# Moving the three steps of the merge statistics to earlier places on VectorE and ScalarE

## The reference, cut to what matters

```python
for g, (window, dil) in enumerate(DILATION_PAIRS):          # (128,1), (512,4), (2048,16)
    o, l = _dilated_group(qkv[:, :, g, 0], qkv[:, :, g, 1], qkv[:, :, g, 2], window, dil, slopes)
    outs.append(o)                                          # l = max + log(sum of exponentials)
    lses.append(l)
wts = jax.nn.softmax(jnp.stack(lses, axis=-1), axis=-1).astype(h.dtype)
o = jnp.einsum('bshg,bshgd->bshd', wts, jnp.stack(outs, axis=3))
y = o.reshape(bsz, s, A_WIDTH) * jax.nn.silu(gate)
return y @ w_out
```

## Time and profile before

| | |
|---|---|
| median of 3 runs | 2000.37 us (1996.89 to 2004.60) |
| the profiled execution, its own time | 2000.56 us |
| its span, first to last instruction | 1998.8 us |
| TensorE busy in the span | 1941.9 us (97%) |
| stretch of the seven pairs whose merge is touched, begin of the first to the last | 183 to 1081 us |
| one pair | 128.3 us |

### The profile page before, as it was taken

The page is one execution under the profiler, slowest core; times in us unless marked ns, Lnnn a source line. Parts: engine busy times, 40 slices in busy tenths (PEclk is TensorE's granted clock), DMA queues, the critical chain, the costliest instruction groups (busy, mean ns, idle before and its releaser), DMA issues.

```text
span 1998.8 us, 33939 instructions
## 1 busy us (share of the span) xinstructions
PE 1941.9 (97%) x12487; PEld 1542.8 (77%) x12487; DVE 1348.5 (67%) x2659; ACT 1051.3 (53%) x2586; POOL 1273.1 (64%) x841
## 2 busy tenths in 40 slices
PE   7999999999999999999999999899999999999998
PEld 4888788787887878877777868687777778777887
DVE  7547667476565765666756867797697598597553
ACT  5454555454555545545454255765765665685320
POOL 0566776866768668687584535575575576586572
PEclk8999999999999999999999999999999999999999
DMA  9111221322213222122135414455454355377431
GB/s 303 48 59 61 77 96 35 101 70 77 85 56 101 70 74 84 61 74 96 48 117 184 169 71 115 142 167 151 130 170 150 127 170 163 121 193 240 171 125 43
DMA packets 117604, 229.50 MB, mean 115 GB/s; under 512 B 22464, under 2 KB 55872, under 8 KB 117440
## 3 DMA queue, kind: packets, MB, share of 16 engines
q1 hardware_dynamic: 117440, 227.32, 36.9%
HBM read 199.42 MB, written 27.86 MB: 114 GB/s over the span
## 4 chain that ended last, share of the span: by engine, by line
PE 71%; DVE 10%; POOL 6%; issue 4%; DMA 3%; ACT 3%; SPq 2%; POOLq 0%; DVEq 0%; ACTq 0%
PE pp L702 24%; PE pp_s L2612 15%; PE po L702 9%; PE tp L787 3%; PE po L863 3%; PE sp_ L775 2%; DVE stage_s L3292 2%; PE yo_p L2816 2%; PE pp_s L2816 2%; PE st_p L2629 2%; POOL qk L634 1%; PE st_p L2816 1%; PE fill L2816 1%; DVE vv L3213 1%; PE yo_p L2644 1%
## 5 line engine op out<-in xcount | busy, mean ns | idle before, releaser
L702 PE MATMUL pp<-h_forms_hi,w_f 128*128 128x512 f32 x1576 | 527.3, 400 | 12.4 <-POOL w_f L589 12.3
L702 PEld LDWEIGHTS pp<-h_forms_hi,w_f 128*128 128x128 f32 x1576 | 297.2, 189 | 82.1 <-POOL w_f L589 21.3
L702 PE MATMUL pp<-h_forms_lo,w_f 128*128 128x512 f32 x788 | 308.1, 391 | 0.0
L589 POOL TENSOR_TENSOR w_f<-w_raw,w_f 128x512 fp32r<-128x512 f32 x154 | 199.9, 1318 | 150.9 <-ACT w_f L1073 150.7
L2612 PE MATMUL pp_s<-h_hi,w_hi_s 128*128 128x512 f32 x624 | 270.2, 433 | 5.2 <-DVE stage_s L3292 2.6
L2612 PE MATMUL pp_s<-h_hi,w_lo_s 128*128 128x512 f32 x624 | 245.7, 394 | 0.0
L2612 PE MATMUL pp_s<-h_lo,w_hi_s 128*128 128x512 f32 x624 | 244.8, 392 | 0.0
L1134 ACT ACTIVATE prob<-prob,mz 128x256 f32<-128x256 f32 (+2 forms) x384 | 169.8, 443 | 110.2 <-DVE mz L1425 109.8
L702 PE MATMUL po<-h_forms_hi,w_f 128*128 128x512 f32 x632 | 208.8, 390 | 0.4 <-POOL w_f L589 0.4
L589 POOL TENSOR_TENSOR w_f<-w_f_raw,w_f 128x512 fp32r<-128x512 f32 x117 | 155.3, 1328 | 79.9 <-ACT w_f L1073 79.9
L702 PEld LDWEIGHTS pp<-h_forms_lo,w_f 128*128 128x128 f32 x788 | 149.2, 189 | 27.6
(11 more groups left out here) (571 smaller groups left out, 4484.9 us busy)
## 6 DMA issues: line engine op xcount, KB each, us to landing
w_raw<-in_a_w SPq DMA_DIRECT2D x80, 512.0 KB, 3.3
rw<-cum_rows SPq DMA_DIRECT2D x32, 1024.0 KB, 6.0
w_raw_s<-in_b_w SPq DMA_DIRECT2D x40, 512.0 KB, 4.5
ew<-exp_rows SPq DMA_DIRECT2D x64, 256.0 KB, 7.0
v<-in_ada_w SPq DMA_DIRECT2D x48, 256.0 KB, 3.3
qk<-merge_rows SPq DMA_DIRECT2D x42, 256.0 KB, 4.3
yT_b<-trunk SPq DMA_DIRECT2D x32, 256.0 KB, 2.6
stage_s<-yT_b SPq DMA_DIRECT2D x14, 512.0 KB, 5.0
```

Source lines behind the costliest of these rows:

```text
L589: return nc.gpsimd.tensor_tensor(out, x, hi.bitcast(F32), ALU.subtract)
L702: last = nc.tensor.matmul(bank, w[:, b], h[:, b], start=b == 0 and t == 0, stop=b == KS - 1 and t == 2)
```

## The change

Three pieces move; nothing is added or removed.

```diff
@@ ScalarE, begin_pair @@
-                    def exponentials():
-                        both(j, 1)
+                    def last_values():
                         if before:
+                            numerators(j - 1, DUOS - 1)
                             shares(j - 1)
 
                     even_step(j, 5 * j + FIRST_UNITS, DUOS_OF_TILES[0], DUOS_OF_TILES[4],
-                              (lambda: numerators(j - 1, DUOS - 1)) if before else nothing, tail_of_pair,
-                              exponentials)
+                              last_values, tail_of_pair, lambda: both(j, 1))
@@ VectorE, loop over the pairs @@
                         elif d == 9:
-                            second_sums(n)
+                            second_sums(n, None, lambda: differences(ch, j))
                         else:
                             second_sums(n, lambda: next_rows(j, d))
                     duo(ch, j + 1, 0)
-                    differences(ch, j)
-                    first_sums(5 * j + (FIRST_UNITS + 5), lambda: shares(ch, j))
+                    shares(ch, j)
+                    first_sums(5 * j + (FIRST_UNITS + 5))
```

## The result

| | before | after |
|---|---|---|
| median of the runs, us | 2000.26 (1996.89 to 2004.60, six runs) | 1984.86 (1982.67 to 1986.63, six runs) |
| profiled execution, us | 2000.56 | 1984.81 |
| its span, us | 1998.8 | 1983.0 |
| TensorE busy in the span | 97% | 98% |

The ratio after to before is 0.992, 95% interval 0.9905 to 0.9935: faster by just under 1%, and clear of noise. It is 15.4 us in the medians and 15.75 us between the two profiled executions.

A forecast was written before the change was run, and what follows sets the result against it. TensorE, 97% busy, was taken as the bound, its waits at unit 5j+8 caused by late shares. 11.1 + 1.2 (transposes' waits) - 1.0 (fourth product) = 11.3 us gained, from 2000.56 to 1989.3 us; range 1985.5 to 1999.5.

The forecast's parts named there:

- The wait at unit 5j+8: TensorE's wait at that unit's first product, for GpSimd's low part, goes because shares land sooner: 11.1 us over seven pairs.
- Differences in front of the last sum: VectorE's last sum moves 2.4 us later, but the delay is hidden from TensorE's third product of unit 5j+7: cost zero.
- The exponential: On ScalarE it runs in idle time; GpSimd's low part of form 3 moves from 600.80 to about 600.1 to 600.2.
- Shares behind the value copies: VectorE's shares end 4.2 us sooner; the copy of b0 delays TensorE's fourth product by 0.15 us, cost 1.0 us.
- The rival of the missed turn: A small VectorE operation falls behind another GpSimd instruction: 1999.5 us in all pairs, 1994 in half; some or all pairs 0.23.
- The landing in front of the last sum: Slower rival: cz lands 1.5 us later, fourth product 3.9 us later per pair: 15 us lost, 2015 us; chance 0.07.
- The reciprocal: Among VectorE's shares, with one SBUF input: not held by GpSimd, 0.54 us; were it held, the fifth operation misses its turn.
- The wait of 1.51 us goes whole: At unit 5j+8's first product, the low part comes 2.4 us sooner, 0.9 us to spare: 11.1 us over seven pairs.
- the fifth operation is not held: Better rival: VectorE's shares end before GpSimd starts form 3: 14.5 us gained, 1986.1 us; chance 0.12.

The follow-up runs named there:

- the late landing: Changed kernel with one statistics transfer sent a second time and waited for before the three cz transfers: 2005.66 us, ratio 1.0023.
- two pairs of kernels: Exponential moved or not: with differences early 1988.59 against 1989.8 us; with b0's copy also ahead of the shares 1978.07 against 1980.58 us.
- the exponential alone: Kernel before with only ScalarE's exponential moved up, VectorE's differences staying behind the value copies: 2010.62 us, ratio 1.0045.
- The delayed kernels: Changed kernel with b0's copy ahead of the shares, plus two cancelling GpSimd operations in the merge: 1988.57 us with 256 columns, 1998.78 us with 512.
- differences and exponential: Changed kernel with VectorE's shares back in their old place, behind the next unit's first two sums: 1988.59 us, ratio 0.9944.
- the wide delay: Changed kernel with b0's copy ahead of the shares, plus two cancelling GpSimd operations of 512 columns in the merge: 1998.78 us, ratio 0.9994.
- the shares alone: Kernel before with only VectorE's shares moved up, right behind the differences, which stay behind the value copies: 2003.39 us, ratio 1.0018.
- the differences alone: Kernel before with only the differences moved in front of VectorE's last sum: 1989.8 us, ratio 0.994.
- the narrow delay: Changed kernel with b0's copy ahead of the shares, plus two cancelling GpSimd operations of 256 columns in the merge: 1988.57 us, ratio 0.9943.
- the copy-first kernel: Changed kernel with VectorE's copy of bank b0 in front of the shares instead of behind them: 1978.07 us, ratio 0.9883.

## Why the prediction was right in its mechanism, and where its size was wrong

**Direction and mechanism.** Right. The wait at unit 5j+8 was the shares' lateness, and it went whole in all seven pairs.

**Differences in front of the last sum.** Right as worked out: cost zero. The wait for the landing is 2.69 us, the three operations take 0.21, 0.21 and 0.35, and nobody on TensorE notices. But the list of those who wait for VectorE there was one short: the value transposes come before the third product, and they are the first to suffer, as the late landing showed.

**The exponential.** Right that it is hidden (two pairs of kernels show no gain from it). Form 3's low part does start 0.69 us sooner in the pair (15.40 us behind the copy `st<-tp`, not 16.09), but the fourth product then waits for the copy of b0, so it did not appear as time.

**Shares behind the value copies.** Right, operation by operation (the first 0.60 us, then held, short, 0.54, held); GpSimd's form 3 starts 2.49 us behind the first share, 2.5 as worked out. They end at 594.25, 3.99 us behind their start, and I had 3.95. The copy of b0 took the blame at the fourth product: in pair 3 it starts 0.85 us behind the product before it, not 0.65 as in the earlier trace rows, so 0.20 us later where I had put 0.15. Over the seven pairs its waits are 3.3 us, 1.24 of it in the last, where VectorE waits 3.81 us for the landing of `cz` instead of 2.69 and hands 0.78 of the 1.12 us on to TensorE. The rival of the missed turn happened in none of the seven pairs: in each the reciprocal starts 0.38 or 0.39 us ahead of GpSimd's form 3.

**The landing in front of the last sum.** The place was right, the price too high. The prediction had 3.9 us a pair for a landing 1.5 us late; 3.35 us late cost 2.3 us of an undisturbed period. In pair 3 there the differences are not held (0.21, 0.21 and 0.34 us), nor are the second and third share (0.21 each).

**The reciprocal.** The doubt is settled. With the late landing it runs from 601.00 to 601.54 beside a GpSimd instruction of 601.01 to 602.29, and neither is lengthened, while the next operation with two operands takes until 602.50. With the exponential alone it starts 0.24 us into a GpSimd instruction (601.46 to 602.80) and still takes 0.54 us:

```profile
601.70 0.54 DVE L1551 RECIPROCAL cm<-cm 32x64 f32<-32x64 f32 x1
```

The rule of the Trainium skill, page "SBUF — State Buffer", section "Who interferes with whom" (one SBUF input outside the 2-port modes does not contend with GpSimd, two inputs do with a GpSimd instruction that reads SBUF), holds in these traces on both sides.

**The size: the step that failed.** "The wait of 1.51 us goes whole" priced the wait at the idle time that the record shows. Taken from the start of the transposes to the first product of unit 5j+8, the stretch was 620.83 - 618.12 = 2.71 us and is 611.81 - 610.96 = 0.85 us. That is 1.86 us, and not 1.51 + 0.17 for the transposes = 1.68. Some 0.27 us more come later in the pair, and 0.20 go at the fourth product of unit 5j+7: 1.93, the measured difference of the periods. Most of the 0.27 is the second lateness of GpSimd's chain, which the prediction had put at nothing. The fourth product of unit 5j+8 stood right behind its low part before (629.18) and has 0.65 us to spare after (619.45). Before:

```profile
629.23 0.50 PE L702 MATMUL pp<-h_forms_hi,w_f 128*128 128x512 f32 x1
```

After:

```profile
620.10 0.39 PE L702 MATMUL pp<-h_forms_hi,w_f 128*128 128x512 f32 x1
```

The delayed kernels show the same from the other side, 0.54 us over the idle time. Against 11.3 / 7 = 1.61 the 1.93 us are 0.32 us more on each of seven pairs, some 2.2 of the 4.2 us that the sum was short of 15.5.

The other 2.0 us are the second pair, where the kernel before loses TensorE's clock behind its wait and the changed kernel does not. The prediction did not look at the granted clock in the stretch of each wait, though the trace of before held it. It counted waits as time lost, not as the cause of slower products behind them.

**The range.** Its better end (1985.5) was the case in which the fifth operation is not held, with the waits at their recorded price. The fifth operation was held, and the gain passed that end by another way. A bound for the price of a wait (between its idle time and some 0.5 us over it, as the delayed kernels show) belonged to the range, and would have moved the end by 2 to 4 us.

## What to carry to other kernels

Take the price of a TensorE wait not from its idle time but from the stretch between two marks on either side, against the same stretch of a pair that does not wait, and look at the granted clock just behind it. Look too at the later products that the same late engine feeds: one can start late without any idle time being listed. Where small steps of another chain are put between large ones, put first what the bounding engine needs next: the same five operations cost nothing behind one copy, and up to 1.2 us in front of it. And when an operation is moved ahead of its input's old arrival, list everyone behind it in order; the first to be late may be one that the old order never made wait.

## What the runs showed of the hardware

- Behind some waits of TensorE of 1.65 us and more the granted clock was near half for about 3 us (some 6 us in three places), and where it was 3 us, 1.0 to 1.8 us were lost beyond the wait. It fell behind one of seven waits in both traces of before (1.29 to 1.76 us), one of six with differences and exponential (at 1.65, not at 1.77), two of seven with the wide delay (1.73 to 3.29), three of seven with the late landing (1.91 to 3.50), five of seven with the shares alone (1.96 to 2.83) and all seven with the exponential alone (2.66 to 3.11). It fell behind none with the differences alone (longest 1.96) or the narrow delay (longest 1.32), and in no pair of the copy-first kernel. Why one wait of 1.7 us brings it on and its neighbour doesn't is open.
- At this place a wait of TensorE costs more than its recorded idle: 1.20 us for 0.66 and 2.30 for 1.75. Of the 0.54 us on top, 0.24 are lost overlap: without a wait the product starts before the recorded end of the transposes in front of it. Most of the rest is a later product that the same chain makes late, and belongs to this kernel.
- A VectorE operation on 32x64 elements with two SBUF operands takes 0.21 us, or up to 1.3 us when a GpSimd instruction is running, and then ends just behind that instruction. If it comes first, it is GpSimd's instruction that gets longer: 1.34 us with the exponential alone (both start at 601.46) against 1.29 us, and 1.41 us after (590.60) beside the first share.
